# Modulation units in a two-block kernel: row units of the first mixer on VectorE, partition sums of four accumulators at a time

## The reference, cut to what matters

```
c_act = silu(c)                                  # 1024 values
mod = c_act @ w_ada[l] + b_ada[l]                # 1024 x 6144
sh1, sc1, g1, sh2, sc2, g2 = split(mod, 6)
h = rms_norm(x, norm1_w) * (1 + sc1) + sh1
x = x + g1 * hybrid_mixer(h, ...)
h = rms_norm(x, norm2_w) * (1 + sc2) + sh2
x = x + g2 * swiglu(h, w_ffn_in, w_ffn_out)
shf, scf = split(c_act @ w_ada_f + b_ada_f, 2)   # 1024 x 2048
```

```
v_new = u_c - w_c @ state
o     = q_c @ state + qk_c @ v_new
state = state * exp(gl) + k_c^T @ v_new
```

## Time and profile before

| | us |
|---|---|
| median of 3 runs (1467.98 to 1469.92) | 1469.01 |
| the profiled execution's own time | 1468.46 |
| its span in the trace | 1466.8 |
| PE busy / VectorE busy / ScalarE busy | 1382.6 / 861.6 / 643.6 |

### The profile page before, as it was taken

How to read it: one execution, slowest core, us unless ns; L and a number is a source line. 1 busy time by engine, 2 the same in 40 slices (tenths; PEclk the granted TensorE clock), 3 DMA queues, 4 the chain that set the end, 5 groups by cost and what they waited for, 6 DMA issues and landing times.

```text
span 1466.8 us, 26588 instructions
## 1 busy us (share of the span) xinstructions
PE 1382.6 (94%) x9971; PEld 1262.4 (86%) x9971; DVE 861.6 (59%) x1635; ACT 643.6 (44%) x1171; POOL 14.9 (1%) x81
## 2 busy tenths in 40 slices
PE   5999999999999899999799987999999999899997
PEld 3988888988888799999678876999997778899996
DVE  0666666766522377777456535777775432775553
ACT  3455544454431255444455423554443231545542
POOL 4000000000000000000000000000000000000000
PEclk9999999999999999999899999999999899899998
DMA  8655536555591078879667912788797263576562
GB/s 305 191 160 157 157 103 186 158 151 165 131 300 46 27 225 260 264 216 294 192 209 223 267 49 72 229 262 263 217 294 246 91 179 98 156 218 174 158 184 87
DMA packets 400020, 270.01 MB, mean 184 GB/s; under 512 B 9914, under 2 KB 357424, under 8 KB 399936
## 3 DMA queue, kind: packets, MB, share of 16 engines
q1 hardware_dynamic: 399936, 268.83, 61.8%
HBM read 267.75 MB, written 1.05 MB: 183 GB/s over the span
## 4 chain that ended last, share of the span: by engine, by line
PE 84%; DVE 8%; ACT 3%; DMA 2%; SPq 2%; issue 2%; DVEq 0%; ACTq 0%
PE bank L743 19%; PE bank L744 18%; PE bank L745 18%; PE bank L729 6%; PE bank L797 4%; PE bank L715 2%; PE bank L695 2%; PE bank L929 1%; PE bank L920 1%; PE bank L689 1%; PE bank L928 1%; DVE w_low L1806 1%; PE bank L1176 1%; DVE h_parts L1822 1%; SPq L523 1%
## 5 line engine op out<-in xcount | busy, mean ns | idle before, releaser
L743 PE MATMUL bank<-h_parts,w_high 128*128 128x256 f32 x1824 | 552.0, 303 | 16.7 <-DVE h_parts L1822 15.0
L744 PE MATMUL bank<-h_parts,w_high 128*128 128x256 f32 x1824 | 522.7, 287 | 0.0
L745 PE MATMUL bank<-h_parts,w_low 128*128 128x256 f32 x1824 | 522.5, 286 | 0.0
L1806 DVE TENSOR_TENSOR w_low<-w_raw,w_high 128x1024 fp32r<-128x1024 f32 (+2 forms) x324 | 361.7, 1124 | 95.9 <-ACT w_high L1321 84.5
L743 PEld LDWEIGHTS bank<-h_parts,w_high 128*128 128x128 f32 x1824 | 355.1, 195 | 34.1 <-issue 23.8
L744 PEld LDWEIGHTS bank<-h_parts,w_high 128*128 128x128 f32 x1824 | 357.3, 196 | 3.6 <-issue 3.4
L745 PEld LDWEIGHTS bank<-h_parts,w_low 128*128 128x128 f32 x1824 | 356.3, 195 | 0.0
L1321 ACT ACTIVATE w_high<-w_raw 128x1024 fp32r<-128x1024 f32 (+2 forms) x324 | 313.1, 973 | 67.4 <-DMA w_raw<-in_ffn_w_out 19.4
L1313 ACT ACTIVATE evac<-bank 128x256 f32<-128x256 f32 x140 | 53.9, 385 | 221.3 <-PE bank L745 195.6
L743 PE MATMUL bank<-act_parts,w_high 128*128 128x256 f32 x528 | 150.1, 284 | 0.0
L744 PE MATMUL bank<-act_parts,w_high 128*128 128x256 f32 x528 | 148.6, 281 | 0.0
(11 more groups left out here) (347 smaller groups left out, 1550.8 us busy)
## 6 DMA issues: line engine op xcount, KB each, us to landing
ada_w<-in_ada_w SPq DMA_DIRECT2D x48, 1024.0 KB, 6.3
w_raw<-in_ffn_w_in SPq DMA_DIRECT2D x88, 512.0 KB, 3.9
w_raw<-in_w_in SPq DMA_DIRECT2D x72, 512.0 KB, 4.0
w_raw<-in_w_ffn_in SPq DMA_DIRECT2D x44, 512.0 KB, 4.0
ada_w<-in_w_ada SPq DMA_DIRECT2D x16, 1024.0 KB, 7.8
w_raw<-in_gla_w_in SPq DMA_DIRECT2D x24, 512.0 KB, 6.4
w_raw<-in_ffn_w_out SPq DMA_DIRECT2D x32, 384.0 KB, 4.1
w_raw<-in_ffn_w_out SPq DMA_DIRECT2D x32, 320.0 KB, 3.6
```

The costliest lines, as they stand in the source:

```text
L743: pe.matmul(acc[:, 0:T], hi[:, n, :], x_parts[:, k, 0, :], start=k == 0, stop=False)
L744: pe.matmul(acc[:, 0:T], hi[:, n, :], x_parts[:, k, 1, :], start=False, stop=False)
L745: mm = pe.matmul(acc[:, 0:T], lo[:, n, :], x_parts[:, k, 0, :], start=False, stop=k == kb - 1)
L1806: dve.tensor_tensor(w_low[:, s, 0:m], w_raw[:, s, 0:m], w_high[:, s, 0:m].bitcast(F32), ALU.subtract)\
```

## The change

1. Row units 1 to 7 of the first mixer leave PE. VectorE accumulates them in head i: multiplication 0 behind level 4, number 1 behind level 5 of the inverse, and numbers 2 to 7 around the first three state updates. Two accumulators `acc2` (the storage of `evac`) take turns; for that VectorE's loop has three passes with two heads in each.
2. Two finished accumulators at a time are summed over the partitions by `acc_rows` in heads 3, 5, 7, and the last one in head 8, behind the first sum (L896) of the head: one 128 x 32 by 128 x 512 matmul for each, in column groups of their own, with a strip of ones in `cact` as the weight. It writes rows of `ADA_BANK` as `ada_rows` did.
3. In the first two feed-forward nets the accumulators of four units are kept (`acc4` in `big`, and `ada_acc` for the fifth) and two `acc_rows` of four matmuls, in round 8 of `hidden` and in the last round of `output`, take the place of eight `unit_sum`. Behind them come one copy, one `ada_sum` and one `ada_bias` in the last round. In the second net, unit 0 keeps a `unit_sum` of its own (`lone`).
4. Loops on PE: `hidden` 0 to 7 one round per pass, round 8 written out, 9 and 10 a loop; in the second net 0 and 1 a loop, 2 written out, 3 to 7, 8, and 9 to 10; `output` 0 to 2 a loop.
5. `ada_copy` of the first mixer waits on `ada_rows`, and a strip of ones is set by GpSimd.

```diff
+            def acc_rows(accs, row0, mac, first=False):
+                pe.wait_ge(S("ada_mac"), mac)
+                for g, acc in enumerate(accs):
+                    row = row0 + g
+                    mm = pe.matmul(ADA_BANK[row_of(g), :], cact[:, 2 * KB, row:row + 32], acc, start=first, stop=True, skip_group_check=True)
+                mm.then_inc(S("ada_rows"), 1)
...
                         if unit is not None and j == 2:
-                            unit_sum(mac + KB * (unit + 1))
+                            unit_sum(mac + KB * (unit + 1), accs=[acc4[:, 0] if lone else ada_acc])
+                        if up4 and j == 2:
+                            acc_rows([acc4[:, u] for u in range(4)], 0, mac + KB * 4, first=True)
...
-                        if unit is not None and j == 2:
-                            unit_sum(mac + KB * (unit + 1))
+                        if down4 and j == 2:
+                            acc_rows([ada_acc[:, :]] + [acc4[:, u] for u in range(3)], 4, mac + KB * 8)
+                        if down4 and j == 5:
+                            ada_sum(mac + KB * 8 + 1)
...
                 pe.matmul(bank[3][:, :], ones[:, :], sq2..., start=True, stop=True).then_inc(S("qk_sum"), 1)
+                if n > 1 and n % 2 or n == H1:
+                    u = (n - 1) // 2 * 2 - 1
+                    acc_rows([acc2[:, 0], acc2[:, 1]] if n < H1 else [acc2[:, 0]], u if n < H1 else H1 - 1, MAC_HEAD + KB * (n - 1))
...
-                        if gemm and c < 3:
-                            ada_rows(A_HEAD + i, 0, i, c - 1)
...
+            def head1(i, gemm, last=False, acc=0):
+                def unit(*ks):
+                    if gemm:
+                        ada_unit(A_HEAD + i, 0, MAC_HEAD + KB * c, ks, acc=acc2[:, acc])
...
+                    if l >= LEVELS - 2:
+                        unit(l - LEVELS + 2)
...
                     if ch < NCH - 1:
+                        unit(2 + 2 * ch)
                         dve.wait_ge(S("s_done"), 3 * c + ch + 1)
                         ... state ...
+                        unit(3 + 2 * ch)
...
-            with dve.Fori(1, H1 - 1) as i:
-                head1(i, True)
+            with dve.Fori(0, H1 // 2 - 1) as p:
+                head1(2 * p + 1, True)
+                head1(2 * p + 2, True, acc=1)
...
-                            units.bias(units.up + units.down - 1)
+                            ada_bias(units.sums + units.lone, units.lone, 8 - units.lone, units.first + units.lone + MOD_UNIT)
...
-                            units.some(units.up + i, [j])
+                            units.some(units.up + i, [j], acc4[:, bass.ds(i, 1), :])
+                        if units and last and j == 4:
+                            ada_copy(units.sums + units.lone, units.accs + 2, "ada_rows")
```

More of the change, by code:

```diff
@@ L758, in hidden @@
                         if unit is not None and j == 2:
-                            unit_sum(mac + KB * (unit + 1))
[L761 to L767, removed]
+                            unit_sum(mac + KB * (unit + 1), accs=[acc4[:, 0] if lone else ada_acc])
+                        if up4 and j == 2:
+                            acc_rows([acc4[:, u] for u in range(4)], 0, mac + KB * 4, first=True)
+                if n_down:
+                    if lone:
+                        with pe.Fori(0, 2) as i:
+                            hidden(i)
+                        hidden(2, unit=0)
+                    with pe.Fori(3 if lone else 0, 8) as i:
+                        hidden(i)
+                    hidden(8, up4=True)
+                    with pe.Fori(9, st_f.n) as i:
+                        hidden(i)
+                else:
+                    for i in range(2):
+                        hidden(i)
+                    with pe.Fori(1, n_up) as p:
+                        hidden(2 * p, p - 1)
+                        hidden(2 * p + 1)
+                    hidden(2 * n_up, n_up - 1)
                     with pe.Fori(2 * n_up + 1, st_f.n) as i:
@@ L770, in ffn, with output @@
                 pe.wait_ge(S("evacuated"), st_d.block0 + 3 - 1)
-                def output(i, last=False, unit=None):
+                def output(i, last=False, down4=False):
                     for j in range(8):
@@ L778, in output @@
                         split_product(st_d, i, j, bank[j // 4], act_parts, OUT_PARTS[j % 4], FB, ready=("act_low", m * FB) if j < 4 else None)
-                        if unit is not None and j == 2:
-                            unit_sum(mac + KB * (unit + 1))
[L782 to L790, removed]
+                        if down4 and j == 2:
+                            acc_rows([ada_acc[:, :]] + [acc4[:, u] for u in range(3)], 4, mac + KB * 8)
+                        if down4 and j == 5:
+                            ada_sum(mac + KB * 8 + 1)
+                with pe.Fori(0, st_d.n - 1) as i:
+                    output(i)
+                output(st_d.n - 1, last=True, down4=n_down > 0)
                 norm_sum(n + 1, range(KB - 2, KB))
@@ L923, in head1 @@
                     if not gemm and l == 2:
-                        ada_sum(2)
+                        ada_sum(MAC_FFN1)
                     pe.wait_ge(S("xs"), 5 * (n - 1) + l)
@@ L987, in _ @@
             ffn(1, st_f1, st_d1, MAC_FFN1, 5, 3)
[L988 removed]
+            pe.wait_ge(S("mod_ready"), 4)
             for h in range(2):
@@ L1763, in _, with ada_copy @@
         def _(dve):
-            def ada_copy(b, used):
-                dve.wait_ge(S("ada_used"), used)
+            def ada_copy(b, used, by="ada_used"):
+                dve.wait_ge(S(by), used)
                 if b:
@@ L1975, in head1 @@
                 if not gemm:
-                    ada_copy(1, 2 * A_FFN1)
+                    ada_copy(1, ACC_HEAD, "ada_rows")
                 dve.wait_ge(S("gb_done"), n)
@@ L2113, in _, with __init__, some @@
             class Units:
-                def __init__(self, first, up, down, c_first, mac, sums):
-                    self.first, self.up, self.down, self.c_first, self.mac, self.sums = first, up, down, c_first, mac, sums
-                def some(self, n, ks):
-                    if ks[0] == 0 and not (isinstance(n, int) and n == 0):
+                def __init__(self, first, up, down, c_first, mac, sums, accs=0, lone=0):
+                    self.lone = lone
+                    self.first, self.up, self.down, self.c_first, self.mac, self.sums, self.accs = first, up, down, c_first, mac, sums, accs
+                def some(self, n, ks, acc=None):
+                    c0 = 0 if isinstance(n, int) and n < self.c_first else KB
+                    if self.down:
+                        if acc is None:
+                            acc = acc4[:, n, :] if n < 4 else ada_acc[:, :]
+                        if ks[0] == 0 and self.lone and isinstance(n, int) and n == 1:
+                            self.bias(0)
+                        if ks[0] == 0 and not isinstance(n, int):
+                            dve.wait_ge(S("ada_rows"), self.accs + 1)
+                        ada_unit(self.first + n, c0, self.mac + KB * n, ks, acc=acc)
+                        return
+                    if ks[0] == 0 and n:
                         self.bias(n - 1)
-                    c0 = 0 if isinstance(n, int) and n < self.c_first else KB
                     ada_unit(self.first + n, c0, self.mac + KB * n, ks, sums=self.sums + n)
```

41 lines of the change are left out of this document (22 added, 19 removed).

## The result

| | before | after |
|---|---|---|
| median, us | 1468.49 (4 runs) | 1448.43 (4 runs, 1441.25 to 1451.66) |
| ratio, 95% interval | | 0.9856 [0.9822, 0.9890] |
| profiled execution: its own time / span, us | 1468.46 / 1466.8 | 1441.25 / 1439.5 |
| PE busy / VectorE busy / ScalarE busy, us | 1382.6 / 861.6 / 643.6 | 1355.4 / 894.9 / 643.2 |

The change is worth 20 us, 1.4%, where 17.0 us (1452.0) was forecast. PE lost 27.2 us of busy time and VectorE gained 33.3. The page of the kernel after: the chain by engine, with 83% for PE, and the costliest group of the multiplications, those into the kept accumulators of the nets, at the 748 ns of the earlier trace rows. With `evac` (49), `ada_acc` (28) and `scratch` (21) as destinations L1806 has 196 instructions where L1784 had 147: seven more in each of seven heads.

A forecast was written before the change was run, and what follows sets the result against it. PE was taken to bound the kernel (84% of the chain). Mixer 9.7, nets 3.8 and 2.9, plus 0.6 for VectorE's waits and loop passes gave 17.0 us off, 1452.0 us against the median; range 1447.5 to 1458.0.

The forecast's parts named there:

- core of 1448.5 to 1455.5: Whole kernel: the forecast's own range in us, from low-clock stretches shifting at about seven places, 3.5 us as random signs.
- Part 2: First mixer: row units as VectorE multiplications delay PE by 0.81 us in six heads, 0.55 in head 7: 5.4 us.
- the 0.6: Nets: 0.6 us gained (0 to 1.2) from VectorE's dropped waits for sums and its halved head-loop passes.
- part 1: First mixer: row units leave PE, 14 halves at 1.20 us each, 16.8 us gained (bounds 14.8 and 16.8).
- part 3: First mixer: `acc_rows` takes 0.96 us; 0.25 counts in heads 3, 5, 7, all in head 8: 1.7 us cost.
- part 4: Feed-forward nets: eight `unit_sum` go for two `acc_rows` and one `ada_sum`, 3.8 us gained; second net 2.9.
- The column groups and the loops: Two rivals: groups in `acc_rows` do not overlap (0.04, 1465 us); more PE loop passes cost fetches (0.02, 1504 us).
- the other signs: Expected profile after: heads of 43.8 us, L2020 0.4 us later, no PE wait before L951, 11.5 us between net rounds.
- The clock: Net starts and similar places: shorter work shifts the 1.2 GHz stretches, 1.3 us at each of about seven, 3.5 us random.
- VectorE later in the state steps than the rows say: Rival, first mixer's state steps: 1 us more per head on the path, gain 7 us smaller, 1459 us; chance 0.15.
- The multiplications as the path: Rival, first mixer: all 5.6 us per head count, 39.5 us in place of 5.4, time 1486 us; chance 0.04.

The follow-up runs named there:

- placed kernel: Changed kernel with multiplications 0 to 3 ahead of level 1 of the inverse, 4 to 7 in the first two state steps: 1442.38 us (0.9821), later 1445.68 (0.9849).
- the fillers: Three matmuls on PE that nobody reads, put before each net's first product in the placed kernel: 1442.97 us, ratio 0.9819.

## Why the prediction was right or wrong

The sign, the place of the gain and the mechanism of the parts that were priced were right; the sum was short. 1448.43 lies in the range of 1447.5 to 1458.0, at its low end, and just under the core of 1448.5 to 1455.5. At equal clock the change is worth 20.6 to 21.6 us where 17.0 were forecast. Two steps failed. Part 2 charged 5.4 us for the multiplications, which cost 3.6; its "There is no idle time to hide it" for number 0 was a misreading of the rows. And the sum put at nothing, without a reason, any change in products whose lines stay the same: the output products of the three nets gained some 2.2 us.

| term | forecast, us | measured, us |
|---|---|---|
| removal of the row units | 16.8 | 15.4 in six stages + 2.39, 17.8 |
| price of the multiplications | 5.4 | 6 x 0.56 + 0.27, 3.6 |
| `acc_rows`, heads 3, 5, 7 and 8 | 1.7 | 3 x 0.43 + 1.17, 2.5 |
| first mixer | 9.7 | 11.7 (`kk` 1 to 8) |
| nets, with the 0.6 | 7.3 | 7.2 (the 4.8 and 3.9 above, less 0.75 each) |
| output products of three nets | 0 | 2.2 |
| sum | 17.0 | 21.1 |

- **Removal** (part 1). The placed kernel, in which PE's gaps in the state steps are those of before, has heads of 42.71 us and so 2.6 less than 45.3, where 2 x 1.20 = 2.40 was taken. The rows' own 1.20 was right: 1.53 us with them, 201.41 - 201.07 = 0.34 now, so 1.19. The rest is the wait for `gmat` before L899, 0.57 to 0.64 us before and 0.37 in the placed kernel. In the sixth stage, where that wait was 0.37 before as well, the gain is 45.09 - 42.71 = 2.38. In the stage from head 7 to head 8 it is 1.22 + 1.17 for the `acc_rows` in it: 2.39, as forecast.
- **Price** (part 2), the mis-sized term. Forecast 0.81 a head; measured 0.56 (43.27 against 42.71), of which 0.22 for number 0 (forecast 0.40) and 0.34 for the rest (0.41). In the last stage it is 45.46 - 45.19 = 0.27 (forecast 0.55). For number 0, I took "L2020 follows `low` directly" to mean that it had no slack. But `low` lets the engine go 1.13 us behind its start (195.97 to 197.10), and L2020 started 1.27 behind it: 0.14 us were free, hidden because neighbouring records overlap. So the copy is 0.26 us late and not 0.40, PE's gap grew by as much (0.18 to 0.43), and the head pays 0.22 to 0.24. The forecast had this number: for number 1 it takes the 1.14 us that `low` holds the engine. Number 1: the gap before L980 (L958 before) grew by 0.19, of the 0.26 named. Numbers 2 to 6 cost nothing, as said. Some 0.1 remain for number 7 (0.15 named), seen as L923's wait of 0.48 against 0.37.
- **`acc_rows`** (part 3). Its 0.96 is 0.98; in heads 3, 5, 7 it adds 0.43 and not 0.25, since the wait for `gmat` that was to hide 0.73 of it was only 0.48 us long by then. In head 8 the stretch from L917 to L923 is 4.62 us where it was 3.45: 1.17, not 0.96. A cover was counted at its old size although another term of the same sum had shrunk it.
- **Luck in the mixer.** The gain by removal was taken 1.0 us too small and the cost of `acc_rows` 0.8 too small; the two nearly cancel.
- **Nets** (part 4). 1.09 for four, forecast 1.20; `ada_sum` 1.03, forecast 0.89. With these sizes the terms give 3.9 and 3.0 us, and 4.1 and 3.2 were measured, so the waits that go, for which 0.6 had been added, were worth 0.3 us or so.
- **Output products.** The forecast took 0.12 us for every product and let it stand. In the output rounds it is 117.8 ns where it was 118.5 to 118.8, and 113.3 where it was 118.7 at the end; the 528 products of a net take 0.75 us less, those of three nets 2.2. What changed it stays open.
- **The column groups and the loops** were as forecast; the runs with one group and with fewer passes show it. L702's four-group call takes 1.07 us by its record (1.06 named), and L708 has 112 records fewer than L695 had. Of the other signs, a head was to last 43.8 us and 0.25 more with `acc_rows`; it lasts 43.27 and 43.70.
- **The clock.** 3.5 us at random was the right size for one execution: 15 of the changed kernel lie between 1441.25 and 1452.36 with a standard deviation of 3.1 us. With the terms put right the forecast would be 1469.0 - 21.1 = 1447.9, and the 1448.43 is well within that. The 3.6 us between 1452.0 and 1448.43 alone, the median of four, could not have told a wrong term from the clock; the stage lengths do.
- **The rivals.** VectorE later in the state steps than the rows say: no, it cost less than forecast. The multiplications as the path: not in the changed kernel, but 4.7 us more of them made it so, at 3.6 us a head (the forecast put the turn to a loss at 3.2 us a head; with 0.56 + 3.6 the kernel is slower than before, 5.5 +- 1.5 us at equal clock). The rival did not name that such waits also bring the clock down, which was a quarter of the loss.

What stays open: why the output products come closer together, and why the second mixer lost time with the fillers.

## What to carry to other kernels

Work moved from the full engine to one with idle time costs its duration only where the idle time is not; read the slack from the distances between starts, with the time that each instruction holds its engine, and not from whether the records touch. When one edit shortens a wait and another hides behind the same wait, count the cover at its new size. When a sum falls short, compare also the stages that the change does not touch. A difference of 0.2% is seen in stage lengths of two profiles at equal clock long before it is seen in medians.

## What the runs showed of the hardware

- Executions of one kernel differ by up to 12 us (1441.25 to 1452.36 for the changed one) in step with how much of them runs at 1.2 GHz: 67 us in one profile of the changed kernel, 80 and 81 in two others. With 10.0 us of it at the start of a net the products take about 1.4 us more than with 3.4 (189.86 against 188.49 us in the second net).
- Where short waits came into dense work, the granted clock fell: with waits of 0.2 to 0.5 us at each state product and one of 1.32, five of the seven stages from `kk` 1 to `kk` 8 got 3.4 or 6.8 us at 1.2 GHz; with only 0.33 and 0.60 at the end of a head, none did in the same stages of the profile after, and one did in another profile of the changed kernel.
- Matmuls of 32 columns in different column groups overlap although each streams its own 128 x 512 tile: two in 0.98 us, four in 1.09; in one group two take 1.83 and four 3.55.
- The distance between the starts of the same products (`act_parts`, 128 x 128 by 128 x 256) was 118.5 to 118.8 ns in one kernel and 117.8, at the end 113.3, in twelve others, at full clock and with unchanged lines: 65.13 against 64.38 us for 528 of them. No run isolates the cause.
